# Twelve more weight panels of a decoder block as split float32r products, and convolution accumulators in PSUM

## The chip, the cores and the metric

The kernel runs on one core of a Trainium2 chip. The metric is the device time of one execution in microseconds; of the kernel before, three executions took 533.55, 533.61 and 533.82 us (median 533.61).

## What is computed

One layer of a hybrid decoder for 256 tokens of width 1024, in float32. A token mixer with two branches, then a mixture of experts:

```python
z = u @ w_in                                   # 1024 x 6144
u_rnn, u_gelu, c_val, c_gate, z_ga, z_gb = split(z)
h   = rg_lru(conv4(u_rnn), ...)                # 4-tap causal convolution, gates, linear recurrence
y_a = (h * gelu(u_gelu)) @ w_rnn_out
c   = conv31(c_val * sigmoid(c_gate))          # 31-tap causal depthwise convolution
y_b = silu(layer_norm(c)) @ w_conf_out
mixed = (sigmoid(z_ga) * y_a + sigmoid(z_gb) * y_b) @ w_out
```

After the mixer come a norm, a router (4 groups of 8 experts, top 2 in the best group) and 32 gated experts of width 256. The mixer is the first 265 us or so of the time, the router and the experts are the rest. The change is in the mixer.

## The kernel before

**Panels.** The mixer's weights are nine matrices of 1024 x 1024, each cut into four panels of 256 output channels, 36 panels `k` of 1 MB. Their order: 0 to 7 alternate between `c_val` (even) and `c_gate` (odd), then `K_RNN` 8 to 11, `K_GELU` 12 to 15, `K_GA` 16 to 19, `K_GB` 20 to 23, `K_YA` 24 to 27, `K_YB` 28 to 31, `K_WOUT` 32 to 35. A panel gives two output chunks `m` of 128 channels, each a sum over 8 blocks of 128 in a PSUM bank (`m % 4`), activation data transposed, 256 tokens as columns.

**Two ways to multiply.** A whole panel (`whole_panel`, L1057, matmuls on L1067) is 16 float32 matmuls of 256 columns, each of which is two records in the trace. A split panel (`split_panel`, `split_products`, L1076 to L1078) first needs its weights cut in two: ACT rounds them to float32r (`weight_hi`, L455, into slot `HI_SLOT + k % 4`), and DVE subtracts this from the original (`weight_lo`, L676, over the original in slot `MIX_SLOT + k % 4`). Then PE does three float32r matmuls in place of one: high by high, high weight by low operand, low weight by high operand. Panels 1, 2, 3 and 16 to 35 are split; 0 and 4 to 15 are whole, the latter in a loop of three turns.

**Loads.** SP issues the load of panel `k` (L328) once PE has finished panel `k - 4` (semaphore `pe_chunk`), since it goes into the same slot. Behind the loads of panels 8 and 10 it also issues expert weights (`load_unit`, four DMAs of 512 KB each time), which lie in slots of their own.

**ACT** evacuates the chunks in the order of the panels: conformer chunks into `cpad` and `gateA` (L448), then the first tap of the 31-tap convolution into `bufC` for two rounds' channels at a time (`first_taps`, L487), recurrence chunks into `bufA` with the first tap of the 4-tap one (L495, L497), gelu chunks into `bufG` (L465). Only at the gelu panels does it begin with the high halves of `K_GA`. After panel 16 come the 16 gate matmuls (`recurrence_gates`, L1109) in banks 4 to 7 in turn, each taken by ACT (L521).

**DVE** runs the 31-tap convolution with two channel blocks in turns (`conv`, L748), `acc = cpad * w + acc`, the accumulator in SBUF (`cacc`), the last tap back into `cpad`. Four rounds `i` of two blocks: rounds 0, 1 and 2 start from `bufC`, with the gating product of the next round (`gated`, L758) before tap 20. Then the 4-tap convolution of all eight blocks (also L748), the low halves of panels 16 and 17, and round 3 (whose tap 0 is L744) with three more low halves between its taps; then the recurrence, norm and more low halves. All of this is one fixed order.

**GpSimd** fills constants until 6.5 us and issues a few DMAs at 25 to 30 us. It does nothing else.

Of the kernel before, what the change touches and what calls it, by code (L numbers as in the profile page):

```python
# [18 lines left out]
F32 = mybir.dt.float32  # L19
# [3 lines left out]
ALU = mybir.AluOpType  # L23
ACT = mybir.ActivationFunctionType
ENG = mybir.EngineType
AX = mybir.AxisListType.X

P = 128
T = 256
TC = T // P  # L30
D = 1024
KC = D // P
CONVW = 31
# [12 lines left out]
PANEL = 2048  # L46
PN = PANEL // KC
SEG = D // PN
NMIX = 9 * SEG
# [9 lines left out]

K_RNN, K_GELU, K_GA, K_GB, K_YA, K_YB, K_WOUT = (n * SEG for n in range(2, 9))  # L60

SPLIT = [1, 2, 3] + list(range(K_GA, NMIX))
HI_SLOT, MIX_SLOT = SEG, 2 * SEG


R_GMIX, R_RCB, R_RCW, R_BR, R_BI, R_A, R_CCB, R_LNG, R_LNB, R_GFFN, R_CCW = 0, 1, 2, 6, 7, 8, 9, 10, 11, 12, 13
# [10 lines left out]
def build(nc, x, g_mix, w_in, rnn_conv_w, rnn_conv_b, lru_w_r, lru_b_r, lru_w_i, lru_b_i, lru_a_param,  # L77
# [4 lines left out]
    mixer_mem = ExitStack()  # L82

    def sb(name, shape, dt=F32, where=None):
        return (where or stack).enter_context(nc.sbuf_tensor(name, shape, dt))

    def loop(engine, lo, hi):

        return nc.Fori(lo, hi, engines=(engine,), hint_back_edge=True)

    def sem(name):
        return stack.enter_context(nc.semaphore(name))

    with stack:
# [36 lines left out]
        rdiag = bufD[:, 0, :].rearrange("p (t a) -> p t a", t=TC)  # L131
        lruw = gateB[:, :, :].rearrange("p (w a) (h j) -> p w (a h) j", w=2, h=2)
        lsc = sb("lsc", [P, 8, KC], F32, mixer_mem)
        cacc = sb("cacc", [P, 2, T], F32, mixer_mem)
        lnw = sb("lnw", [P, 3, T], F32, mixer_mem)
        mixer_mem.close()
        moe_mem = stack
# [46 lines left out]
        act_std = sem("act_std")  # L184
        act_whi = sem("act_whi")
        dve_wlo = sem("dve_wlo")
        act_split = sem("act_split")
        dve_split = sem("dve_split")
        act_lexp = sem("act_lexp")
# [4 lines left out]
        pe_chunk = sem("pe_chunk")  # L194
# [176 lines left out]
        def _(gp):  # L371
# [42 lines left out]
            gp.dma_start(brt[:, 0:NG], bcast(b_group_router, 0, P)).then_inc(router_in, 16)  # L414
            gp.dma_start(brt[:, NG:], bcast(b_expert_router, 0, P)).then_inc(router_in, 16)


        @block.scalar
        def _(act):
# [19 lines left out]
                act.activation(actT[:, c, :], ps[:, c % 4, c // 4 * T:(c // 4 + 1) * T], ACT.Copy,  # L439
                               scale=par[:, c, R_GMIX:R_GMIX + 1]).then_inc(act_evac, 1)  # L440

            def take_conformer(i):

                for b in range(4):
                    act.wait_ge(pe_chunk, i * 4 + (KC + b + 1))
                    c = bass.ds(i * 2 + b % 2, 1)
                    d = cpad[:, c, CONVW - 1:] if b < 2 else gateA[:, c, :]
                    act.activation(d.rearrange("p a b -> p (a b)"), ps[:, b, 0:T],  # L448
                                   ACT.Copy if b < 2 else ACT.Sigmoid).then_inc(act_evac, 1)

            def weight_hi(k):


                act.wait_ge(mixw_full[k % SEG], 16 * (k // SEG + 1))
                act.activation(ring_r[:, HI_SLOT + k % SEG, :], ring[:, MIX_SLOT + k % SEG, :], ACT.Copy  # L455
                               ).then_inc(act_whi, 1)

            def take_panel(k, func, dst, before=None):

                for m in (2 * k, 2 * k + 1):  # L460
                    c = m % KC
                    act.wait_ge(pe_chunk, KC + m + 1)
                    if before:
                        before(c)
                    act.activation(dst[:, c, 0:T], ps[:, m % 4, 0:T], func).then_inc(act_evac, 1)  # L465
# [18 lines left out]
            def first_taps(i):  # L484
                act.wait_ge(dve_cmul, i * 2 + 2)
                for c in (2 * i, 2 * i + 1):
                    act.activation(bufC[:, c, :], cpad[:, c, 0:T], ACT.Identity, scale=par[:, c, R_CCW:R_CCW + 1],  # L487
                                   bias=par[:, c, R_CCB:R_CCB + 1]).then_inc(act_ctap, 1)

            def take_rnn(i):  # L490

                for b in range(4):
                    c = i * 4 + b
                    act.wait_ge(pe_chunk, 3 * KC + c + 1)
                    act.activation(bufA[:, c, RNNW - 1:], ps[:, b, 0:T], ACT.Copy).then_inc(act_evac, 1)  # L495
                    act.wait_ge(act_evac, 3 * KC + c + 1)
                    act.activation(bufB[:, c, :], bufA[:, c, 0:T], ACT.Identity, scale=par[:, c, R_RCW:R_RCW + 1],  # L497
                                   bias=par[:, c, R_RCB:R_RCB + 1]).then_inc(act_tap, 1)

            act.wait_ge(gp_step, 7)  # L500
            take_conformer(0)
            first_taps(0)
            with loop(ENG.Activation, 1, SEG - 1) as i:
                take_conformer(i)
            first_taps(1)
            take_conformer(SEG - 1)
            first_taps(2)
            take_rnn(0)
            take_rnn(1)
            for p in range(SEG):  # L510
                if p >= 2:
                    weight_hi(K_GA + p - 2)
                take_panel(K_GELU + p, ACT.Gelu_apprx_tanh, bufG)
            weight_hi(K_GA + 2)
            take_ga(0)

            for m in range(2 * KC):
                c, w = m // 2, m % 2
                act.wait_ge(pe_lru, m + 1)
                row = (R_BR, R_BI)[w]  # L520
                act.activation((bufC, bufD)[w][:, c, :], ps[:, 4 + m % 4, 0:T], ACT.Sigmoid,  # L521
                               bias=par[:, c, row:row + 1]).then_inc(act_lru, 1)
            weight_hi(K_GA + 3)

# [137 lines left out]
        def _(v):  # L662
# [97 lines left out]

            def conformer_conv(lo, hi, before, **how):

                conv(lo, hi, cpad, lambda c, j: cacc[:, j:j + 1, :], lambda c, j: cpad[:, c, CONVW - 1:],
                     CONVW, R_CCW, R_CCB, before, dve_conv, **how)

            v.wait_ge(gp_step, 14)
# [261 lines left out]
        def _(pe):  # L1028
# [28 lines left out]
            def whole_panel(s, p, first=False):  # L1057

                pe.wait_ge(mixw_full[p], s * 16 + 16)
                w = slot_kn(ring, MIX_SLOT + p)  # L1060
                for m in (2 * p, 2 * p + 1):

                    pe.wait_ge(act_evac, s * KC + max(KC + m - 3, KC))
                    for k in range(KC):
                        if first:
                            pe.wait_ge(dve_u, k + 1)
                        last = pe.matmul(ps[:, m % 4, 0:T], w[:, k, (m % 2) * P:(m % 2 + 1) * P],  # L1067
                                         actT[:, k, :], start=(k == 0), stop=(k == KC - 1))
                    last.then_inc(pe_chunk, 1)
# [10 lines left out]

            def split_panel(k, x_hi, x_lo, before):

                pe.wait_ge(dve_wlo, SPLIT.index(k) + 1)
                w_hi, w_lo = slot_kn(ring_r, HI_SLOT + k % SEG), slot_kn(ring_r, MIX_SLOT + k % SEG)
                for m in (2 * k, 2 * k + 1):
                    before(m)
                    cols = slice((m % 2) * P, (m % 2 + 1) * P)
                    split_products(ps[:, m % 4, 0:T], lambda c: w_hi[:, c, cols], lambda c: w_lo[:, c, cols],
                                   lambda c: x_hi[:, c, 0:T], lambda c: x_lo[:, c, 0:T]).then_inc(pe_chunk, 1)
# [3 lines left out]

            whole_panel(0, 0, first=True)
            pe.wait_ge(dve_split, 1)
            for k in SPLIT[:3]:
                split_panel(k, u_hi, u_lo, evac_bank)
            with loop(ENG.PE, 1, K_GA // SEG) as s:
                for p in range(SEG):
                    whole_panel(s, p)  # L1100
            def recurrence_gates():
                pe.wait_ge(lruw_in, 32)
                for m in range(2 * KC):
                    c, w = m // 2, m % 2
                    if w == 0:
                        pe.wait_ge(dve_conv4, c + 1)
                    if m >= 4:
                        pe.wait_ge(act_lru, m - 3)
                    pe.matmul(ps[:, 4 + m % 4, 0:T], lruw[:, w, c, :], bufB[:, c, :], start=True, stop=True  # L1109
                              ).then_inc(pe_lru, 1)  # L1110

            def channel_sums(src, bank):
# [48 lines left out]
                return last  # L1161

            for p in range(SEG):
                pe.wait_ge(dve_wlo, SPLIT.index(K_WOUT + p) + 1)
                w_hi, w_lo = slot_kn(ring_r, HI_SLOT + p), slot_kn(ring_r, MIX_SLOT + p)
                for tc in range(TC):
                    if p:
                        pe.wait_ge(dve_h, 2 * (p - 1) + tc + 1)
                    tok = slice(tc * P, (tc + 1) * P)
                    split_products(ps[:, 4 + tc, 0:PN], lambda k: bufA_r[:, k, tok], lambda k: gateA_r[:, k, tok],  # L1170
                                   lambda k: w_hi[:, k, :], lambda k: w_lo[:, k, :],

                                   before=(lambda k: pe.wait_ge(dve_split, 4 + k + 1)) if p == tc == 0 else None
                                   ).then_inc(pe_wout, 1)
                if p >= 1:
                    h_transposes(p - 1)
                if p == 2:
                    pe.wait_ge(dve_gw, KC)
                if p >= 2:
                    logits(p - 2)  # L1180
# [163 lines left out]
```

## Time and profile before

| | us |
|---|---|
| median of the runs | 533.61 |
| span of the profiled execution, first to last instruction | 531.7 |
| PE busy, share of the span | 509.5, 96% |
| DVE busy | 273.2, 51% |
| ACT busy | 209.2, 39% |
| GpSimd busy | 9.6, 2% |

The total of the profiled execution is not listed beside its span; the median lies 1.9 us above the span. The page averages over the mixer and the experts; the windows and the order of time, which the rows below are from, show them apart. Matmul records overlap, since they are pipelined: their spacing, not their length, is what one costs. `issue` as a releaser means that the profile shows nothing that the engine waited for.

### The profile page before, as it was taken

The page shows a single profiled execution, that of the slowest core. Times are in us where ns is not written, and L with a number is a line of the kernel's source. Part 1 is how long each engine was busy: PE and PEld are TensorE (multiplying, and loading weights), DVE is VectorE, ACT ScalarE, POOL GpSimd, SP SyncE. Part 2 cuts the span into 40 slices and gives each one's busy share as a digit, 9 for nine tenths or more (in the row PEclk, how much of TensorE's full clock was granted, in tenths as well). Part 3 has the DMA queues.
Part 4 walks back from the last instruction along what each step waited for, and adds up shares of the span by engine and source line. Part 5 has one row for each costly group of instructions (what it writes and reads, how often), then busy time and mean ns, then how long its engine had stood idle before and what let it go on. Part 6 is the DMA issues. An engine that isn't in the chain of part 4 may idle for free.

```text
span 531.7 us, 8105 instructions
## 1 busy us (share of the span) xinstructions
PE 509.5 (96%) x2983; PEld 359.7 (68%) x2983; DVE 273.2 (51%) x550; ACT 209.2 (39%) x315; POOL 9.6 (2%) x25
## 2 busy tenths in 40 slices
PE   4999999999999999999989999999999999999994
PEld 4998888888999999999964353535435353534531
DVE  0589999969999996678282202221221212122123
ACT  2561113323897779345243231412323141322414
POOL 3020000000000000000000000000000000000000
PEclk8799999999999999999999999999999999999998
DMA  7594995434444438759996999999999999999932
GB/s 238 171 250 159 300 301 182 141 125 146 152 154 163 158 109 283 244 166 326 322 387 248 363 361 373 372 350 369 356 367 372 372 361 359 372 372 369 355 137 79
DMA packets 115970, 143.31 MB, mean 270 GB/s; under 512 B 3934, under 2 KB 106398, under 8 KB 115946
## 3 DMA queue, kind: packets, MB, share of 16 engines
q1 hardware_dynamic: 115502, 141.75, 79.5%
q0 software_dynamic: 432, 1.21, 0.8%
q8 instruction: 16, 0.26, 0.2%
q14 instruction: 8, 0.07, 0.0%
q10 hardware_dynamic: 12, 0.02, 0.0%
HBM read 141.90 MB, written 1.05 MB: 269 GB/s over the span
## 4 chain that ended last, share of the span: by engine, by line
PE 90%; DVE 4%; ACT 3%; DMA 2%; issue 1%; SPq 0%; DVEq 0%; ACTq 0%
PE ps L1267 21%; PE ps L1067 17%; PE ps L1304 11%; PE ps L1076 7%; PE ps L1078 7%; PE ps L1077 7%; PE ps L1219 6%; PE ps L1250 6%; DMA bufB<-in_conf_conv_b 2%; PE ps L1114 1%; PE ps L1109 1%; DVE ring_r L676 1%; PE ps L1032 1%; PE ps L1277 1%; PE ps L1286 1%; ACT bufC L565 1%
## 5 line engine op out<-in xcount | busy, mean ns | idle before, releaser
L1067 PE MATMUL ps<-actT,ring 128*128 128x256 f32 x416 | 90.8, 380 | 1.5 <-ACT gateA L448 1.0
L748 DVE SCALAR_TENSOR_TENSOR cacc<-cpad,par,cacc 128x256 f32<-128x256 f32 x226 | 90.3, 477 | 0.0
L1067 PEld LDWEIGHTS ps<-actT,ring 128*128 128x128 f32 x416 | 78.7, 190 | 13.1 <-ACT gateA L448 1.6
L1267 PE MATMUL ps<-ring,xslot 128*64 128x512 f32 x384 | 85.1, 594 | 0.0
L975 DVE SCALAR_TENSOR_TENSOR y_lo<-ps,wslot,y_hi 128x1024 fp32r<-128x1024 f32 x16 | 20.5, 1284 | 105.6 <-ACT y_hi L624 105.6
L1267 PEld LDWEIGHTS ps<-ring,xslot 128*64 128x64 f32 x384 | 27.0, 137 | 52.2 <-issue 51.4
L676 DVE TENSOR_TENSOR ring_r<-ring,ring_r 128x2048 fp32r<-128x2048 f32 x23 | 52.1, 2284 | 1.4 <-ACT ring_r L455 1.3
L1076 PE MATMUL ps<-u_hi,ring_r 128*128 128x256 f32 x176 | 50.4, 286 | 0.7 <-issue 0.7
L1077 PE MATMUL ps<-u_lo,ring_r 128*128 128x256 f32 x176 | 49.8, 283 | 0.0
L1078 PE MATMUL ps<-u_hi,ring_r 128*128 128x256 f32 x176 | 49.8, 283 | 0.0
L455 ACT ACTIVATE ring_r<-ring 128x2048 fp32r<-128x2048 f32 x23 | 43.7, 1907 | 8.4 <-DMA ring<-in_w_rnn_out 2.7
L987 DVE TENSOR_REDUCE wslot<-ps 64x1 f32<-64x2 f32 x32 | 5.1, 158 | 73.7 <-PE ps L1277 73.2
L638 ACT ACTIVATE sgate<-ps 128x256 f32<-128x256 f32 x16 | 6.1, 384 | 79.0 <-PE ps L1267 79.0
L1304 PE MATMUL ps<-ring,hidT 128*64 128x512 f32 x160 | 36.5, 598 | 0.0
L1076 PEld LDWEIGHTS ps<-u_hi,ring_r 128*128 128x128 f32 x176 | 33.8, 192 | 1.2 <-issue 1.1
L1077 PEld LDWEIGHTS ps<-u_lo,ring_r 128*128 128x128 f32 x176 | 33.8, 192 | 0.1
L1078 PEld LDWEIGHTS ps<-u_hi,ring_r 128*128 128x128 f32 x176 | 33.8, 192 | 0.0
L633 ACT ACTIVATE xslot<-ps 128x512 f32<-128x512 f32 x32 | 19.1, 598 | 37.1 <-PE ps L1250 37.1
L624 ACT ACTIVATE y_hi<-ps,wslot 128x1024 fp32r<-128x1024 f32 x16 | 17.8, 1111 | 35.7 <-PE ps L1304 35.7
L1267 PE MATMUL ps<-ring_high,xslot 128*64 128x512 f32 x128 | 28.6, 594 | 0.0
L1250 PE MATMUL ps<-sel,hn_hi 128*128 128x256 f32 x128 | 26.6, 289 | 1.3 <-DVE hn_lo L871 1.3
L1250 PE MATMUL ps<-sel,hn_lo 128*128 128x256 f32 x128 | 25.6, 282 | 0.0
(230 smaller groups left out, 775.6 us busy)
## 6 DMA issues: line engine op xcount, KB each, us to landing
ring<-in_w_in SPq DMA_DIRECT2D x24, 1024.0 KB, 5.2
ring<-in_w_gate SPq DMA_DIRECT2D x48, 512.0 KB, 8.8
ring<-in_w_up SPq DMA_DIRECT2D x48, 512.0 KB, 8.9
ring<-in_w_down SPq DMA_DIRECT2D x40, 512.0 KB, 8.1
ring_high<-in_w_gate SPq DMA_DIRECT2D x16, 512.0 KB, 8.9
ring_high<-in_w_up SPq DMA_DIRECT2D x16, 512.0 KB, 9.0
ring_high<-in_w_down SPq DMA_DIRECT2D x16, 512.0 KB, 8.2
ring<-in_w_rnn_out SPq DMA_DIRECT2D x4, 1024.0 KB, 4.9
```

The costliest lines, as they stand in the source:

```text
L455: act.activation(ring_r[:, HI_SLOT + k % SEG, :], ring[:, MIX_SLOT + k % SEG, :], ACT.Copy).then_inc(act_whi, 1)
L676: v.tensor_tensor(ring_r[:, MIX_SLOT + k % SEG, :], ring[:, MIX_SLOT + k % SEG, :], ring_r[:, HI_SLOT + k % SEG, :].bitcast(F32), ALU.subt ...
L748: ins = v.scalar_tensor_tensor(out=d if k == taps - 1 else a, in0=s, scalar=w, in1=start(c) if start and k == first else a, op0=ALU.mult, ...
L975: v.scalar_tensor_tensor(out=y_lo[:, :], in0=ps[:, 6:8, :].rearrange("p a b -> p (a b)"), scalar=wslot[:, pair:pair + 1], in1=y_hi[:, :].b ...
L1067: last = pe.matmul(ps[:, m % 4, 0:T], w[:, k, (m % 2) * P:(m % 2 + 1) * P], actT[:, k, :], start=(k == 0), stop=(k == KC - 1))
L1076: pe.matmul(dst, w_hi(k), x_hi(k), start=(k == 0), stop=False)
L1077: pe.matmul(dst, w_hi(k), x_lo(k), start=False, stop=False)
L1078: last = pe.matmul(dst, w_lo(k), x_hi(k), start=False, stop=(k == KC - 1))
L1219: last = pe.matmul(ps[:, 2 * tc + nn, :], selT[:, pair, tc * P:(tc + 1) * P], y[:, nn * 512:(nn + 1) * 512], start=False, stop=stop, skip_ ...
L1250: last = pe.matmul(ps[:, 4 + c // 2 % 2, c % 2 * T:(c % 2 + 1) * T], part[:, tc, c * P:(c + 1) * P], sel[:, tc, :], start=(t == 0), stop=( ...
L1267: last = pe.matmul(ps[SLOTS * j:SLOTS * (j + 1), 4, :], xslot[:, k, e * SLOTS:(e + 1) * SLOTS], w, start=(k == 0), stop=(k == KC - 1), ski ...
L1304: last = pe.matmul(ps[SLOTS * j:SLOTS * (j + 1), 6 + nn, :], hidT[:, f, SLOTS * j:SLOTS * (j + 1)], w[:, f, nn * 512:(nn + 1) * 512], star ...
```

## The change

Panels 4 to 15 become split panels. For them ACT makes the high half as for the others, and GpSimd the low half, in two instructions of 1024 columns each. ACT makes the high half of panel `k + 3` after it has evacuated panel `k`. PE's loop over the three groups of whole panels becomes straight code, as does ACT's loop over the conformer panels. The accumulators of the 31-tap convolution move from SBUF to bank 7 of PSUM, and the gate matmuls therefore take turns in banks 4 to 6. DVE's instructions and their order are the same otherwise.

```diff
-SPLIT = [1, 2, 3] + list(range(K_GA, NMIX))
+SPLIT = list(range(1, NMIX))
+
+POOL_LO = range(SEG, K_GA)
+DVE_LO = [k for k in SPLIT if k not in POOL_LO]
 HI_SLOT, MIX_SLOT = SEG, 2 * SEG
+GATE_BANKS, ACC_BANK = 3, 7
+WLO_PARTS = 2
...
-        cacc = sb("cacc", [P, 2, T], F32, mixer_mem)
...
+            for k in POOL_LO:
+                gp.wait_ge(act_whi, SPLIT.index(k) + 1)
+                for part in range(WLO_PARTS):
+                    cols = slice(part * PANEL // WLO_PARTS, (part + 1) * PANEL // WLO_PARTS)
+                    gp.tensor_tensor(ring_r[:, MIX_SLOT + k % SEG, cols], ring[:, MIX_SLOT + k % SEG, cols],
+                                     ring_r[:, HI_SLOT + k % SEG, cols].bitcast(F32), ALU.subtract
+                                     ).then_inc(gp_wlo, 1)
...
             act.wait_ge(gp_step, 7)
-            take_conformer(0)
-            first_taps(0)
-            with loop(ENG.Activation, 1, SEG - 1) as i:
-                take_conformer(i)
-            first_taps(1)
-            take_conformer(SEG - 1)
-            first_taps(2)
-            take_rnn(0)
-            take_rnn(1)
-            for p in range(SEG):
-                if p >= 2:
-                    weight_hi(K_GA + p - 2)
-                take_panel(K_GELU + p, ACT.Gelu_apprx_tanh, bufG)
-            weight_hi(K_GA + 2)
+            for k in range(K_GA):
+                if k < K_RNN:
+                    take_conformer(k)
+                elif k < K_GELU:
+                    take_rnn(k - K_RNN)
+                else:
+                    take_panel(k, ACT.Gelu_apprx_tanh, bufG)
+                if k == 1:
+                    first_taps(0)
+                if k == 5:
+                    first_taps(1)
+                if k == K_RNN + 2:
+                    first_taps(2)
+                if k >= 1:
+                    weight_hi(k + 3)
             take_ga(0)
...
-                conv(lo, hi, cpad, lambda c, j: cacc[:, j:j + 1, :], lambda c, j: cpad[:, c, CONVW - 1:],
+                def conv_acc(j):
+                    return ps[:, ACC_BANK, j * T:(j + 1) * T].rearrange("p (a b) -> p a b", a=1)
+                conv(lo, hi, cpad, lambda c, j: conv_acc(j), lambda c, j: cpad[:, c, CONVW - 1:],
                      CONVW, R_CCW, R_CCB, before, dve_conv, **how)
...
-                pe.wait_ge(dve_wlo, SPLIT.index(k) + 1)
+                if k in POOL_LO:
+                    pe.wait_ge(gp_wlo, WLO_PARTS * (POOL_LO.index(k) + 1))
+                else:
+                    pe.wait_ge(dve_wlo, DVE_LO.index(k) + 1)
...
-            for k in SPLIT[:3]:
+            for k in range(1, K_GA):
                 split_panel(k, u_hi, u_lo, evac_bank)
-            with loop(ENG.PE, 1, K_GA // SEG) as s:
-                for p in range(SEG):
-                    whole_panel(s, p)
...
-                    if m >= 4:
-                        pe.wait_ge(act_lru, m - 3)
-                    pe.matmul(ps[:, 4 + m % 4, 0:T], lruw[:, w, c, :], bufB[:, c, :], start=True, stop=True
+                    if m >= GATE_BANKS:
+                        pe.wait_ge(act_lru, m - GATE_BANKS + 1)
+                    pe.matmul(ps[:, 4 + m % GATE_BANKS, 0:T], lruw[:, w, c, :], bufB[:, c, :], start=True, stop=True
                               ).then_inc(pe_lru, 1)
```

## Rows read from the trace of the kernel before

**Rows 1.** The page: busy us, share of the span, instructions of each engine.
```profile
PE 509.5 (96%) x2983; PEld 359.7 (68%) x2983; DVE 273.2 (51%) x550; ACT 209.2 (39%) x315; POOL 9.6 (2%) x25
```

**Rows 2.** Chain of waits in order of time: start us, us, what.
```profile
46.55 27.91 PE ps L1067 x128
...
74.92 27.91 PE ps L1067 x128
...
103.28 27.89 PE ps L1067 x128
```

**Rows 3.** Windows after the twelve panels: busy us (instructions), granted clock, DMA share, GB/s.
```profile
130.00:140.00 10.00, 10.00 (x70) 9.48 (x68) 10.00 (x18) 6.85 (x12) 0.00 (x0) 1.00 0.50 159
...
sum 70.00, PE 69.97 PEld 67.97 DVE 68.72 ACT 55.60 POOL 0.00; mean PE 10.00 PEld 9.71 DVE 9.82 ACT 7.94 POOL 0.00
```

**Rows 4.** Order of time on DVE: start us, us, what, [idle before <-releaser].
```profile
37.77 0.88 DVE L748 SCALAR_TENSOR_TENSOR cacc<-cpad,par,bufC 128x256 f32<-128x256 f32 x2 [1.16 <-ACT bufC L487]
...
63.50 14.33 DVE L748 SCALAR_TENSOR_TENSOR cacc<-cpad,par,cacc 128x256 f32<-128x256 f32 x36
...
111.22 0.87 DVE L748 SCALAR_TENSOR_TENSOR cpad<-cpad,par,cacc 128x256 f32 x2
117.08 10.26 DVE L748 SCALAR_TENSOR_TENSOR bufB<-bufA,par,bufB  x24 [4.99 <-issue]
127.26 4.49 DVE L676 TENSOR_TENSOR ring_r<-ring,ring_r 128x2048 fp32r<-128x2048 f32 x2
```

**Rows 5.** Order of time on ACT: ends of panels 1, 3, 15, and two gates.
```profile
34.51 0.38 ACT L448 ACTIVATE gateA<-ps 128x256 f32<-128x256 f32 x1 [1.46 <-PE ps L1078]
...
46.11 0.38 ACT L448 ACTIVATE gateA<-ps 128x256 f32 x1 [2.49 <-PE ps L1078]
...
131.21 0.39 ACT L465 ACTIVATE bufG<-ps 128x256 f32<-128x256 f32 x1 [3.07 <-PE ps L1067]
...
137.40 0.47 ACT L521 ACTIVATE bufC<-ps,par 128x256 f32<-128x256 f32 x1
137.83 0.48 ACT L521 ACTIVATE bufD<-ps,par 128x256 f32<-128x256 f32 x1
```

**Rows 6.** PE's early pause, and windows around it, columns as in rows 3.
```profile
5.01 2.56 PE L1040 MATMUL ps<-ident,hres 128*128 128x128 f32 x16
13.79 1.08 PE L1046 MATMUL ps<-ident,bufB 44*128 44x44 f32 x8 [6.22 <-DMA bufB<-in_conf_conv_b]
...
10.00:12.00 2.00, 0.00 (x0) 0.00 (x0) 0.00 (x0) 0.00 (x0) 0.00 (x0) 0.50 0.91 276
...
18.00:20.00 2.00, 2.00 (x11) 2.00 (x11) 1.35 (x4) 0.56 (x2) 0.00 (x0) 0.51 1.09 354
20.00:22.00 2.00, 2.00 (x15) 1.85 (x14) 1.97 (x8) 0.12 (x1) 0.00 (x0) 1.00 0.28 91
```

**Rows 7.** Order of time on DVE, operations with SBUF and PSUM inputs.
```profile
276.21 1.39 DVE L871 SCALAR_TENSOR_TENSOR hn_lo<-hg,stat,hn_hi 128x512 fp32r<-128x512 f32 x2
...
516.17 0.42 DVE L990 TENSOR_TENSOR hid<-sgate,ps 128x256 f32<-128x256 f32 x1
516.51 0.75 DVE L928 TENSOR_TENSOR sel<-rank,iota_s 128x256 fp32r<-128x256 f32 x2
...
525.87 1.41 DVE L1022 SCALAR_TENSOR_TENSOR hres<-ps,stat,gfin 128x512 f32<-128x512 f32 x2
```

**Rows 8.** GpSimd in order of time; DVE beside its DMA issues; ACT's high halves.
```profile
3.97 1.49 POOL L397 TENSOR_SCALAR selT<-ones 128x512 fp32r<-128x512 f32 x1
...
26.38 0.90 POOL L411 DMA_DIRECT2D gateB<-in_lru_w_i  x1
...
26.10 6.69 DVE L676 TENSOR_TENSOR ring_r<-ring,ring_r 128x2048 fp32r<-128x2048 f32 x3
...
L455 ACT ACTIVATE ring_r<-ring 128x2048 fp32r<-128x2048 f32 x23 | 43.7, 1907 | 8.4 <-DMA ring<-in_w_rnn_out 2.7
```

**Rows 9.** DMA queues in 114 to 115 us: packets, MB, share.
```profile
q14 instruction: 1, 0.01, 2.3%
```

**Rows 10.** DMA issues of weight panels: count, KB each, median us to landing.
```profile
ring<-in_w_in SPq DMA_DIRECT2D x24, 1024.0 KB, 5.2
```

More of the change, by code:

```diff
@@ L186, in build @@
         dve_wlo = sem("dve_wlo")
+        gp_wlo = sem("gp_wlo")
         act_split = sem("act_split")
@@ L440, in _, with take_conformer @@
                                scale=par[:, c, R_GMIX:R_GMIX + 1]).then_inc(act_evac, 1)
[L442 to L449, printed above, removed]
+            def take_conformer(k):
+                for j in range(2):
+                    c = k // 2 * 2 + j
+                    act.wait_ge(pe_chunk, KC + 2 * k + j + 1)
+                    d = cpad[:, c, CONVW - 1:] if k % 2 == 0 else gateA[:, c, :]
+                    act.activation(d, ps[:, (2 * k + j) % 4, 0:T], ACT.Copy if k % 2 == 0 else ACT.Sigmoid
+                                   ).then_inc(act_evac, 1)
             def weight_hi(k):
@@ L490, in take_rnn @@
             def take_rnn(i):
-                for b in range(4):
-                    c = i * 4 + b
+                for c in (2 * i, 2 * i + 1):
+                    b = c % 4
                     act.wait_ge(pe_chunk, 3 * KC + c + 1)
@@ L520, in _ @@
                 row = (R_BR, R_BI)[w]
-                act.activation((bufC, bufD)[w][:, c, :], ps[:, 4 + m % 4, 0:T], ACT.Sigmoid,
+                act.activation((bufC, bufD)[w][:, c, :], ps[:, 4 + m % GATE_BANKS, 0:T], ACT.Sigmoid,
                                bias=par[:, c, row:row + 1]).then_inc(act_lru, 1)
@@ L1163, in _ @@
             for p in range(SEG):
-                pe.wait_ge(dve_wlo, SPLIT.index(K_WOUT + p) + 1)
+                pe.wait_ge(dve_wlo, DVE_LO.index(K_WOUT + p) + 1)
                 w_hi, w_lo = slot_kn(ring_r, HI_SLOT + p), slot_kn(ring_r, MIX_SLOT + p)
```

## Prediction

> **What bounds the kernel now.** I read the page first [rows 1]: PE is busy 509.5 of 531.7 us, DVE 273.2. An average over two quite different halves says little, so I next took the chain of waits for the mixer half [rows 2]: three blocks of 27.9 us of float32 matmuls (L1067) follow one another, 46.55 to 131.2, and each is four of the twelve panels that the change touches. After them PE goes on without a pause: in the seven windows from 130 to 200 us it is busy 69.97 of 70.00 us [rows 3]. So PE is the bound from 28.5 us on. The question is who is second, and how far behind. DVE's order of time [rows 4] answers it: DVE is convolving without a gap from 37.8 to 112.1 us, has one gap of 4.99 us, does the 4-tap convolution to 127.3, then the low half of panel K_GA (L676), and its other windows up to 190 us are full too [rows 3]. DVE is a second chain, running beside PE and almost as long.
>
> **The twelve panels.** Panel 15, the last float32 one, is evacuated at 131.21; panel 3, the last split one, at 46.11; panel 1 at 34.51 [rows 5]. So twelve float32 panels take 85.1 us, and one split panel takes (46.11 - 34.51) / 2 = 5.80 us. Twelve split panels would take 69.6 us, and PE would have finished panel 15 at 46.1 + 69.6 = 115.7 instead of 131.2: 15.5 us less work.
>
> **Who ends the wait for panel K_GA.** The first thing PE needs next is the low half of panel K_GA, and DVE makes it, after its convolutions, in an order that the diff leaves alone. DVE's first L676 of that pair starts at 127.26 and takes 2.28 us: 129.5 [rows 4]. Nothing on DVE's way there is taken off it: the twelve new low halves are GpSimd's, but the old kernel did not have them at all. DVE also waits for nobody on that way who becomes faster, since its only idle time there is the 4.99 us with no releaser. So PE can start K_GA at 129.5, only 131.2 - 129.5 = 1.7 us earlier; the other 13.8 us of the saving become a wait. Term one: -1.7 us.
>
> **What the wait itself costs.** At the start of the kernel PE stops at 7.57 us, and the granted clock is 0.50 from 10 us on; PE resumes at 13.79 and has the full clock only from about 20.0 [rows 6]. That is a level of 1.2 GHz instead of 2.4 for 6.2 us of work, which loses 3.1 us. A wait of 13.8 us is longer than that pause of 6.2, so panel K_GA and the first gates would run at the lower level. Behind them PE was full already [rows 3], so nothing absorbs it. Bounds 0 and 3.1; I take 3.1, the row. Term two: +3.1 us.
>
> **What happens to DVE's convolution.** Three pieces.
> - Accumulators in PSUM. Up to 112.1 us DVE issues 174 operations that write the accumulator (29 taps, 2 channels, 3 rounds), spaced (14.34 - 0.48) / 35 = 0.396 us [rows 4]. No row has DVE writing to PSUM. As a source, PSUM costs a scalar_tensor_tensor of 512 columns 12 ns: two in a row take 1.41 us from PSUM and 1.39 with both inputs in SBUF, and single ones 746 against 738 ns; the tensor_tensor of 256 columns with a PSUM input is followed after 0.34 us, as those from SBUF are [rows 7]. So 0 to 12 ns on the input side, I take 6: 1.0 us. The output side is bounded by the two spacings that this engine shows at 256 columns, 0.34 and 0.40: one operation could be 60 ns shorter (-10 us) or, as far again the other way, 60 ns longer (+10 us). A result has to be written either way; I take nothing.
> - Meeting GpSimd. GpSimd would now read and write SBUF for 60 us beside DVE. The trace has no such overlap: GpSimd computes until 6.5 us, and what it does at 26 to 30 us are DMA issues, beside which DVE's 2048-column subtractions take their usual 2.2 us each [rows 8]. Lower bound 0. Upper bound: DVE operations with both inputs in SBUF wait out whatever GpSimd instruction is running. While GpSimd works there are five such pairs (the gating at taps 20 of three rounds, and the first tap from bufC in two). GpSimd's only 512-column arithmetic takes 1.49 us [rows 8], so half a panel is at least 2.98 us, and catching it half way costs 1.5 us: 7.5 us. I take 3, a little under the middle.
> - The gap of 4.99 us. An instruction packet lands in 114 to 115 us on the queue that fetched for DVE [rows 9], with a weight load under way; this is code, and its length stays. Between 0 and -5 us; I take 0.
>
> Term three: +1.0 + 3.0 = +4.0 us.
>
> **What is hidden.** Everything that feeds the twelve panels has 13.8 us of cover. ACT's twelve more high halves cost it 1.9 us of each 5.8 [rows 8], beside two evacuations of 0.38 [rows 5]. Weight loads land in 5.2 us at the median, under the 5.8 of a panel [rows 10]; the two unit loads of 2 MB, which SP issues behind the loads of K_RNN and K_RNN + 2, push the next panel load back some 6 us each, and the cover takes that. PE's unrolled code is straight-line, as in K_GA to K_GB, where it runs at full rate [rows 3]. The gates' banks go from four to three: ACT takes one gate each 0.43 us at 0.47 us a piece [rows 5], PE needs 0.43, so a bank is back after 0.90 of the 1.29 us that three give. If there is no wait before K_GA (DVE much faster) these would begin to show, at most 2 us.
>
> GpSimd is cover-dependent too. Its first low half can start at 39.6 (ACT free at 37.7, 1.9 for the high half); it is hidden while 39.6 + 12p + 5.8 is under 133.5, that is while a panel takes it p < 7.3 us. From the row above p is at least 4 x 1.49 = 5.96, and twice that if a second input costs as much as the first. The Trainium skill, GPSIMD Engine Reference, Performance versus the Vector engine, gives 4497 ns for a float32 tensor_tensor of 2048 columns; by it GpSimd would keep up even with 5.8 us a panel. That row of 1.49 us for a quarter of the columns doesn't agree well with it.
>
> **Sum.** -1.7 + 3.1 + 4.0 = +5.4 us. Of the profiled execution, whose span is 531.7, that makes 537.1; its own total isn't listed, and the median of the runs is 1.9 above the span, so 533.6 + 5.4 = 539.0 us. From K_GA on PE is late by 5.4 and DVE by 4.0 (+0.4 for 58 further PSUM operations), so PE stays the bound and hands the whole of it to the expert half.
>
> **Rivals.**
> - A, faster: DVE reaches K_GA earlier. The place is the 174 operations; it decides as soon as terms two and three together are below +1.7, so with no meeting cost when an operation gets over 8 ns shorter (1.4 / 174). With 20 ns (-3.5), 2 us off the code gap and nothing lost to GpSimd: 1.4 - 5.5 = -4.1, 529.5 us. For: the gap depends on what is in the DMA queues, and 0.34 us is shown for an operation of that length. Against: PSUM rows are never shorter. 0.20.
> - B, GpSimd bounds. At 9 us a panel (between 5.96 and 11.9) the last low half is at 39.6 + 108 = 147.6, PE starts K_GA at 153.4, +22.2: 555.8 us. For: the 1.49 us row. 0.12.
> - C, the convolution keeps its pace and GpSimd does not disturb it: 1.4 us, 535.0. For: the tensor_tensor rows. 0.15, half of it inside 0.2%.
> - D, full exclusion: 1.4 + 1.0 + 7.5 = +9.9, 543.5 us. DVE's paired operations wait for whole GpSimd halves, five times. 0.13.
>
> By the Trainium skill, SBUF — State Buffer, Who interferes with whom, a VectorE instruction with two SBUF inputs and a GpSimd instruction that reads SBUF exclude each other, and the later one waits for the whole instruction; one with a single SBUF input does not. By that rule it would be D, and the accumulators in PSUM would spare the other taps. No row here shows it.
>
> **The numbers.** My own sum 0.40, A 0.20, B 0.12, C 0.15, D 0.13. A measurement of this kernel tells changes above 0.2% (1.1 us). Slower: 0.40 + 0.12 + 0.13 + 0.07 = 0.72; the same 0.08; faster 0.20. The range goes down to 530, which holds half of A, and up to 548, which holds D and a convolution some 50 ns slower an operation, and leaves B out.
>
> **What would show it.** PE idle before K_GA for 10 us or more, ended by DVE ring_r L676 (step one), with the granted clock at 0.5 for some 6 us after (step two). DVE's spacing in the convolution, 0.396 us or other; longer first taps or gatings while POOL is busy (step three). POOL's time for half a panel: over 3.6 us is B. I am wrong if DVE's first low half of K_GA comes before 128 us, or if the clock holds through the wait.

## The result and the profile after

The changed kernel took 540.04 us (median of four runs, 539.01 to 543.72) against 533.58 us in the same session: ratio 1.0125, 95% interval 1.0104 to 1.0146. It is slower, by 6.5 us; 539.0 was forecast. The profiled execution took 540.59 us with a span of 538.5, 6.8 us above the span of before.

The page of the changed kernel, first part and the rows of the slices for PE, GpSimd and the clock:

```profile
PE 499.6 (93%) x3175; PEld 358.7 (67%) x3175; DVE 278.5 (52%) x550; ACT 230.4 (43%) x327; POOL 67.3 (12%) x49
...
PE   4999999950999999999999999999999999999994
...
POOL 3139779800000000000000000000000000000000
PEclk8799999995899999999989999999999999999999
```

PE has 10 us less to do than in [rows 1] and the kernel is longer: for half of slice 9 and nearly all of slice 10 PE stands idle, and the granted clock falls to a half. The waits name who ended that:

```profile
PE ps L1092 <- DVE ring_r L690: 19.7, 2, 19.1
```

One wait of 19.1 us for a low half from DVE. Line numbers are higher by 13 to 16 now: L690 is the low half on DVE, L762 the taps, L772 the gating, L468 the high half. The order of time on DVE, which answers [rows 4]:

```profile
52.70 1.81 DVE L772 TENSOR_TENSOR cpad<-cpad,gateA 128x256 f32<-128x256 f32 x2
...
63.55 2.73 DVE L762 SCALAR_TENSOR_TENSOR ps<-cpad,par,bufC 128x256 f32 x2 [0.42 <-DVE cpad L762]
66.20 14.19 DVE L762 SCALAR_TENSOR_TENSOR ps<-cpad,par,ps 128x256 f32<-128x256 f32 x36
...
90.04 3.81 DVE L762 SCALAR_TENSOR_TENSOR ps<-cpad,par,bufC 128x256 f32 x2 [0.38 <-DVE cpad L762]
...
121.99 10.25 DVE L762 SCALAR_TENSOR_TENSOR bufB<-bufA,par,bufB  x24 [4.75 <-issue]
132.16 4.48 DVE L690 TENSOR_TENSOR ring_r<-ring,ring_r 128x2048 fp32r<-128x2048 f32 x2
```

Taps with the accumulator in PSUM take 14.19 us for 36, where [rows 4] has 14.33. But pairs of operations with both inputs in SBUF take up to 3.81 us; in the kernel before such a pair took 0.75 (gating) or 0.88 us (first taps). I call what a pair takes above that what it lost: here 1.06, 1.85 and 2.93, together 5.8 us. The other two of the five pairs fell into stretches in which GpSimd had nothing to do. DVE comes to its low halves at 132.16 instead of 127.26. ACT's evacuations, which answer [rows 5]: ends of panels 1, 3, 15 and K_GA, and K_YA:

```profile
34.56 0.38 ACT L461 ACTIVATE gateA<-ps 128x256 f32<-128x256 f32 x1 [1.46 <-PE ps L1094]
...
46.08 0.38 ACT L461 ACTIVATE gateA<-ps 128x256 f32<-128x256 f32 x1 [2.50 <-PE ps L1094]
...
115.44 0.38 ACT L478 ACTIVATE bufG<-ps 128x256 f32<-128x256 f32 x1 [2.49 <-PE ps L1094]
...
142.92 0.38 ACT L478 ACTIVATE gateA<-ps 128x256 f32<-128x256 f32 x1 [2.52 <-PE ps L1094]
...
202.82 0.39 ACT L478 ACTIVATE bufD<-ps 128x256 f32<-128x256 f32 x1 [2.24 <-PE ps L1094]
```

Panel 15 is finished at 115.44, K_GA at 142.92 (136.96 before), K_YA at 202.82 (197.05 before). GpSimd in order of time, with its 24 new instructions:

```profile
39.65 14.25 POOL L426 TENSOR_TENSOR ring_r<-ring,ring_r 128x1024 fp32r<-128x1024 f32 x6 [9.40 <-ACT ring_r L468]
54.11 5.04 POOL L426 TENSOR_TENSOR ring_r<-ring,ring_r 128x1024 fp32r<-128x1024 f32 x2 [0.21 <-ACT ring_r L468]
```

14.25 us for six is 2.38 us a half panel, under the 2.98 that was forecast as its least. And the clock, which answers [rows 6] (columns as in [rows 3]):

```profile
118.00:120.00 2.00, 0.00 (x0) 0.00 (x0) 0.00 (x0) 0.93 (x1) 0.00 (x0) 0.86 0.95 332
120.00:122.00 2.00, 0.00 (x0) 0.00 (x0) 0.01 (x1) 0.00 (x0) 0.00 (x0) 0.50 0.01 2
...
138.00:140.00 2.00, 2.00 (x12) 2.00 (x11) 2.00 (x6) 0.00 (x0) 0.00 (x0) 0.52 0.00 0
140.00:142.00 2.00, 2.00 (x18) 2.00 (x18) 2.00 (x3) 0.39 (x1) 0.00 (x0) 1.00 0.00 0
```

PE resumed at 134.5 and had 1.2 GHz until 140, 5.5 us.

Of the 6.8 us, 5.8 are there at K_YA (202.82 against 197.05) and still at the router's logits (273.15 against 267.40). The last 1.1 us arise behind them, in 273 to 277 us, where eight matmuls on the residual take 4.96 instead of 3.59 us, the granted clock being 0.50 there:

```profile
274.00:275.00 1.00, 1.00 (x2) 0.40 (x2) 0.83 (x7) 1.00 (x1) 0.00 (x0) 0.50 0.99 290
```

The kernel before had 1.00 in the same stage of its profile. I have no experiment on this dip, and its cause stays open. But it isn't the new panels that bring it: the kernel before with nothing changed but its accumulators and gate banks (second experiment) shows it in its profile, and two kernels with the new panels (quarters with pauses, and the same with 80 matmuls on constants) do not:

```profile
268.00:270.00 2.00, 2.00 (x5) 1.19 (x5) 1.61 (x11) 1.98 (x2) 0.00 (x0) 0.51 0.96 311
```

### The profile page after: what moved, and what is told of

It reads as the page before. It is cut to its first block, busy times and chain, and to the rows that moved or that the text cites. A ratio compares the mean times of both kernels' runs of the same rounds, so it can differ in the third digit from the quotient of the medians.

```text
span 538.5 us, 8483 instructions
## 1 busy us (share of the span) xinstructions
PE 499.6 (93%) x3175; PEld 358.7 (67%) x3175; DVE 278.5 (52%) x550; ACT 230.4 (43%) x327; POOL 67.3 (12%) x49
## 4 chain that ended last, share of the span: by engine, by line
PE 70%; DVE 16%; issue 6%; ACT 3%; DMA 2%; DVEq 2%; SPq 0%
PE ps L1283 21%; PE ps L1320 11%; DVE ps L762 9%; PE ps L1092 6%; PE ps L1235 6%; PE ps L1093 6%; PE ps L1094 6%; PE ps L1266 6%; DVE ring_r L690 3%; DMA bufB<-in_conf_conv_b 2%; PE ps L1125 1%; PE ps L1130 1%; DVEq L761 1%; PE ps L1293 1%; PE ps L1212 1%
## 5 line engine op out<-in xcount | busy, mean ns | idle before, releaser
L1092 PE MATMUL ps<-u_hi,ring_r 128*128 128x256 f32 x368 | 106.0, 288 | 19.6 <-DVE ring_r L690 19.1
L1094 PE MATMUL ps<-u_hi,ring_r 128*128 128x256 f32 x368 | 105.2, 286 | 0.0
L1093 PE MATMUL ps<-u_lo,ring_r 128*128 128x256 f32 x368 | 105.2, 286 | 0.0
L762 DVE SCALAR_TENSOR_TENSOR ps<-cpad,par,ps 128x256 f32<-128x256 f32 x226 | 89.4, 479 | 0.0
L1092 PEld LDWEIGHTS ps<-u_hi,ring_r 128*128 128x128 f32 x368 | 71.8, 195 | 20.4 <-DVE ring_r L690 19.3
L468 ACT ACTIVATE ring_r<-ring 128x2048 fp32r<-128x2048 f32 x35 | 66.5, 1907 | 15.3 <-DMA ring<-in_w_in 8.5
L1093 PEld LDWEIGHTS ps<-u_lo,ring_r 128*128 128x128 f32 x368 | 71.8, 195 | 0.1
L1094 PEld LDWEIGHTS ps<-u_hi,ring_r 128*128 128x128 f32 x368 | 71.7, 195 | 0.0
L426 POOL TENSOR_TENSOR ring_r<-ring,ring_r 128x1024 fp32r<-128x1024 f32 x24 | 57.7, 2443 | 17.7 <-ACT ring_r L468 17.7
L690 DVE TENSOR_TENSOR ring_r<-ring,ring_r 128x2048 fp32r<-128x2048 f32 x23 | 52.1, 2284 | 0.5 <-ACT ring_r L468 0.4
L647 ACT ACTIVATE xslot<-ps 128x512 f32<-128x512 f32 x32 | 19.1, 598 | 37.0 <-PE ps L1266 37.0
L1266 PEld LDWEIGHTS ps<-sel,hn_hi 128*128 128x128 f32 x128 | 19.6, 189 | 7.2 <-issue 7.2
```

The lines of the kernel that those rows point to most:

```text
L426: gp.tensor_tensor(ring_r[:, MIX_SLOT + k % SEG, cols], ring[:, MIX_SLOT + k % SEG, cols], ring_r[:, HI_SLOT + k % SEG, cols].bitcast(F32) ...
L690: v.tensor_tensor(ring_r[:, MIX_SLOT + k % SEG, :], ring[:, MIX_SLOT + k % SEG, :], ring_r[:, HI_SLOT + k % SEG, :].bitcast(F32), ALU.subt ...
L762: ins = v.scalar_tensor_tensor(out=d if k == taps - 1 else a, in0=s, scalar=w, in1=start(c) if start and k == first else a, op0=ALU.mult, ...
L1092: pe.matmul(dst, w_hi(k), x_hi(k), start=(k == 0), stop=False)
L1093: pe.matmul(dst, w_hi(k), x_lo(k), start=False, stop=False)
L1094: last = pe.matmul(dst, w_lo(k), x_hi(k), start=False, stop=(k == KC - 1))
```

## The experiments

Twelve kernels. Times are medians; a ratio is to the kernel before in the same session, with its 95% interval.

**Accumulators in SBUF again.** The changed kernel with this undone:

```diff
+        cacc = sb("cacc", [P, 2, T], F32, mixer_mem)
-                conv(lo, hi, cpad, lambda c, j: conv_acc(j), ...
+                conv(lo, hi, cpad, lambda c, j: cacc[:, j:j + 1, :], ...
```

> The changed kernel with the 31-tap accumulators back in SBUF, GpSimd still making the twelve low halves. Theory (a DVE operation with both inputs in SBUF and a GpSimd instruction exclude each other, for the length of the instruction): every tap now has two SBUF inputs, so nearly each of GpSimd's 24 instructions of 2.4 us holds DVE up once. DVE's convolution gets some 50 us longer while GpSimd works, K_GA starts that much later, 580 to 595 us. Rival (the 5.8 us that the five pairs lost have another cause, such as the start of a tensor_tensor): the taps keep 0.39 us and the time stays within 2 us of 540.

583.18 us, ratio 1.0919 (1.0896 to 1.0943). The theory held: DVE comes to its 4-tap convolution 44 us later than in the changed kernel (166.28 against 121.99). DVE and GpSimd in order of time:

```profile
38.46 14.34 DVE L763 SCALAR_TENSOR_TENSOR cacc<-cpad,par,cacc 128x256 f32<-128x256 f32 x36
...
53.39 29.32 DVE L763 SCALAR_TENSOR_TENSOR cacc<-cpad,par,cacc 128x256 f32<-128x256 f32 x20
...
41.15 32.24 POOL L427 TENSOR_TENSOR ring_r<-ring,ring_r 128x1024 fp32r<-128x1024 f32 x8 [10.64 <-ACT ring_r L469]
```

One detail was not in the theory. From 41.15 GpSimd had work, yet DVE's 36 taps went on at full pace to 52.8 us, and GpSimd's first instruction took 14.53 us. Then the engines took turns: DVE's next 20 taps took 29.3 instead of 8 us, and taken singly, 24 operations of DVE waited behind GpSimd's 24 instructions, one behind each. So DVE's stream of short operations kept GpSimd out, but GpSimd's stream of long ones did not keep DVE out. The first eight GpSimd instructions took 32.2 us in place of 19.

**Accumulators in PSUM alone.** The kernel before with them in bank 7 and the gates in three banks:

```diff
+GATE_BANKS, ACC_BANK = 3, 7
-                conv(lo, hi, cpad, lambda c, j: cacc[:, j:j + 1, :], ...
+                conv(lo, hi, cpad, lambda c, j: conv_acc(j), ...
-                    pe.matmul(ps[:, 4 + m % 4, 0:T], ...
+                    pe.matmul(ps[:, 4 + m % GATE_BANKS, 0:T], ...
```

> The kernel before with the accumulators in PSUM bank 7 and the gates in three banks, nothing else. Theory: taps are 4 ns shorter each (14.19 against 14.33 us for 36), DVE reaches K_GA 0.7 us earlier, PE is the bound there and nothing moves: 533.6 within 0.3 us. Rival: three gate banks or PSUM writes cost something by themselves: 534.5 to 536.

533.89 us, ratio 0.9996 (0.9984 to 1.0008). Taps 14.19 us for 36 in each round, so it is PSUM and not GpSimd's company that makes them 4 ns shorter. Neither that nor the three banks moves the time.

**Matmuls on constants in the wait**, to keep the clock up. This was tried four times, until it bridged the wait:

```diff
+            keep_warm(80)
+
             def recurrence_gates():
```

> The changed kernel with 80 float32 matmuls of 128 columns on constants between panel 15 and K_GA, 17 us of work in a wait of 19. Theory (the wait costs the clock): granted clock 1.00 through K_GA, panel K_GA takes 5.8 instead of 8.4 us, 537.3 us. Rival (the clock stretch is absorbed behind): 540 as before.

540.46 us, ratio 1.0106 (1.0057 to 1.0156): undecided. In the profiled run DVE's pairs lost 10.8 us instead of 5.8, PE began K_GA at 138.5, the constants ended at 133.5, and the clock had fallen again. The runs lay between 538.3 and 543.1: what the pairs lose differs from run to run, and had to be made steady first.

**Length of GpSimd's instructions.** One of 2048 columns a panel, and eight of 256:

```diff
-WLO_PARTS = 2
+WLO_PARTS = 1      # and, in the next kernel, 8
```

> The changed kernel with GpSimd's low half as one instruction of 2048 columns per panel (some 4.7 us) instead of two of 2.4. Theory (DVE's pairs with two SBUF inputs wait for the end of the running instruction): what they lose grows with the instruction's length, from 5.8 and 10.8 us in the two profiles of two halves to 10 to 18 us; 544 to 552 us, with a wide spread. Rival (a fixed cost for each meeting): 538 to 543 as with two halves.

552.25 us, ratio 1.0341 (1.0326 to 1.0356). The time is 0.3 us above the expected range; 20.4 us were lost in the pairs, where 10 to 18 were expected.

> The changed kernel with GpSimd's low half as eight instructions of 256 columns. Theory: no pair waits more than some 0.7 us an operation, together 2 to 4 us instead of 5.8 to 10.8, the low half of K_GA comes near 131, and the time is 535.5 to 538 us with a spread under 2 us. Rival (a fixed cost for each meeting, or as many more meetings as the instructions are shorter): 540 or more. GpSimd may need some 0.1 to 0.2 us more an instruction, up to 6 us a panel, which PE's wait covers.

549.22 us (543.83 to 550.12), ratio 1.0283 (1.0268 to 1.0298). Missed: short instructions are hardly better than long ones. With one instruction a panel, the two operations of a pair on DVE and GpSimd's instructions beside them, taken singly:

```profile
82.76 3.31 DVE L772 TENSOR_TENSOR cpad<-cpad,gateA  x1
85.99 4.84 DVE L772 TENSOR_TENSOR cpad<-cpad,gateA  x1
...
81.16 4.63 POOL L426 TENSOR_TENSOR ring_r<-ring,ring_r 128x2048 fp32r<-128x2048 f32 x1 [2.79 <-ACT ring_r L468]
85.75 4.80 POOL L426 TENSOR_TENSOR ring_r<-ring,ring_r 128x2048 fp32r<-128x2048 f32 x1
```

GpSimd's instructions end at 85.79 and 90.55, DVE's operations at 86.07 and 90.83. Each operation of the pair waits for the end of the instruction that is running when it comes: the first for what is left of one, the second, since GpSimd has begun again meanwhile, for a whole further one. In the changed kernel, with halves, it is the same. GpSimd's instructions beside this pair end at 91.03 and 93.57:

```profile
90.04 1.27 DVE L762 SCALAR_TENSOR_TENSOR ps<-cpad,par,bufC 128x256 f32 x1 [0.38 <-DVE cpad L762]
91.23 2.62 DVE L762 SCALAR_TENSOR_TENSOR ps<-cpad,par,bufC 128x256 f32 x1
```

In the five profiles with instructions of 1024 or 2048 columns 46 operations waited, and all 46 ended 0.28 to 0.30 us after the first end of a GpSimd instruction that came behind their start. With eight:

```profile
52.55 9.97 DVE L772 TENSOR_TENSOR cpad<-cpad,gateA 128x256 f32<-128x256 f32 x1
...
39.83 22.40 POOL L426 TENSOR_TENSOR ring_r<-ring,ring_r 128x256 fp32r<-128x256 f32 x32 [9.77 <-ACT ring_r L468]
```

An instruction takes 0.70 us, and DVE's operation nevertheless took 9.97. It let 13 ends of instructions pass and ended at 62.52, where GpSimd's stream of 32, for four panels without a break, had ended at 62.23. The other four waits of this profile were one instruction long. So behind short instructions an operation sometimes waits until GpSimd's stream pauses; what decides whether it does, no run shows. With eight, a panel takes GpSimd 5.6 us, as long as a panel of PE, and pauses become rare. My theory fell in this point. The profiled execution was the fastest of the five, 543.83 us; the next kernel's profile shows what the others may have lost.

> As the kernel with eight instructions a panel, and 62 float32 matmuls of 128 columns on constants (13.6 us) between panel 15 and K_GA. With the short instructions K_GA's low half should come within 2 us of the last of them, before the clock falls. Theory (the wait costs 2.7 to 3.1 us of clock): 2.5 to 3 us less than that kernel without them, 533 to 535 us. Rival (the stretch is absorbed): the same time as without them.

549.87 us, ratio 1.0277 (1.0244 to 1.0310). Two operations waited to the end of GpSimd's streams, 10.36 and 7.06 us; the pairs lost 17.7 us, so it doesn't tell of the clock.

**A pause behind each instruction.** Quarters, and GpSimd waits for its own semaphore:

```diff
-WLO_PARTS = 2
+WLO_PARTS = 4
                                      ).then_inc(gp_wlo, 1)
+                    gp.wait_ge(gp_wlo, WLO_PARTS * POOL_LO.index(k) + part + 1)
```

> The changed kernel with four instructions a panel on GpSimd, and GpSimd waiting for its own semaphore after each, so that its stream pauses. Theory formed on the traces of one and of eight instructions a panel (DVE's two-input operation waits until GpSimd's back-to-back stream pauses, 9.7 us in one case, not until the running instruction ends): with a pause behind each instruction of 1.26 us no pair loses more than 1.3 us an operation, together 3 to 6 us, against 5.8 to 10.8 in halves and 11 to 16 in eighths; 536 to 540 us with a small spread. Rival (many short instructions are themselves what costs): 544 to 550 us, as with eighths. GpSimd needs 5.4 to 5.8 us a panel.

539.51 us, ratio 1.0101 (1.0086 to 1.0117), all four runs between 539.01 and 539.84. The time is as the theory had it; the pairs:

```profile
52.60 2.61 DVE L773 TENSOR_TENSOR cpad<-cpad,gateA 128x256 f32<-128x256 f32 x2
...
64.25 2.09 DVE L763 SCALAR_TENSOR_TENSOR ps<-cpad,par,bufC 128x256 f32 x2 [0.42 <-DVE cpad L763]
...
90.10 2.28 DVE L763 SCALAR_TENSOR_TENSOR ps<-cpad,par,bufC 128x256 f32 x2 [0.38 <-DVE cpad L763]
...
39.84 27.65 POOL L426 TENSOR_TENSOR ring_r<-ring,ring_r 128x512 fp32r<-128x512 f32 x20 [9.73 <-ACT ring_r L469]
```

GpSimd is at work for 27.65 us with hardly a gap, and yet no pair loses more than 1.9 us. Together they lose 6.3, a little above what I expected, and the four runs lie within 0.8 us. This run changed the length and the pause together, and by itself it doesn't show what the pause does: a wait of one instruction of 1.3 us an operation would look the same without it. The pair of kernels that differs in the pause alone comes last.

> The same, with 66 float32 matmuls of 128 columns on constants (14.5 us) between panel 15 and K_GA. Theory (the wait costs clock): granted clock 1.00 at the start of K_GA and 2.5 to 3 us less than without them. Rival (absorbed): no difference.

539.93 us, ratio 1.0102 (1.0086 to 1.0117). The constants ended at 130.6, the clock was at 0.50 from 134 on, K_GA came at 134.9: not bridged, so the last run used 80.

> The kernel with four instructions a panel, the pause behind each, and 80 instead of 66 matmuls on constants before K_GA: with 66 the last of them ended at 130.6 us, the clock fell near 133.7, and K_GA came at 134.9, so that run did not bridge the wait. 80 of 0.223 us end at 133.7, 1.2 us before K_GA. Theory (the wait costs clock): granted clock 1.00 through K_GA, its panel in 5.8 instead of 8.2 to 8.4 us, and 2.4 to 3 us less than the 539.5 us without them: 536.5 to 537.2. Rival (the stretch at the lower level is absorbed behind): 539 to 540.

538.96 us, ratio 1.0100 (1.0084 to 1.0117), against 1.0101 without the constants. The wait was bridged this time:

```profile
134.00:136.00 2.00, 1.11 (x9) 1.11 (x10) 2.00 (x2) 0.00 (x0) 0.00 (x0) 1.00 0.00 0
136.00:138.00 2.00, 2.00 (x19) 2.00 (x19) 2.00 (x4) 0.00 (x0) 0.00 (x0) 1.00 0.00 0
```

The rival is right for this kernel: the stretch at the lower clock is absorbed. ACT's evacuations at K_GA and K_YA with the clock held, and then without (the kernel of the pauses alone):

```profile
140.94 0.38 ACT L479 ACTIVATE gateA<-ps 128x256 f32<-128x256 f32 x1 [2.49 <-PE ps L1095]
...
202.36 0.38 ACT L479 ACTIVATE bufD<-ps 128x256 f32<-128x256 f32 x1 [1.82 <-PE ps L1095]
```

```profile
142.48 0.38 ACT L479 ACTIVATE gateA<-ps 128x256 f32<-128x256 f32 x1 [2.49 <-PE ps L1095]
...
202.37 0.39 ACT L479 ACTIVATE bufD<-ps 128x256 f32<-128x256 f32 x1 [1.96 <-PE ps L1095]
```

PE is 1.54 us ahead at K_GA and 0.01 at K_YA. With the clock held it waits 0.8 us on the way, for ACT's squares of the layer norm, which ACT makes from DVE's subtraction of the mean. This subtraction in the kernel before, the changed kernel, with 66 and with 80 matmuls, and then K_GA and K_YA with 66:

```profile
183.32 2.29 DVE L812 TENSOR_TENSOR cpad<-cpad,lnw 128x2048 f32<-128x2048 f32 x1
...
188.21 2.30 DVE L828 TENSOR_TENSOR cpad<-cpad,lnw 128x2048 f32<-128x2048 f32 x1
...
188.63 2.29 DVE L829 TENSOR_TENSOR cpad<-cpad,lnw 128x2048 f32<-128x2048 f32 x1
...
188.61 2.29 DVE L829 TENSOR_TENSOR cpad<-cpad,lnw 128x2048 f32<-128x2048 f32 x1
...
143.34 0.39 ACT L479 ACTIVATE gateA<-ps 128x256 f32<-128x256 f32 x1 [2.51 <-PE ps L1095]
...
203.23 0.39 ACT L479 ACTIVATE bufD<-ps 128x256 f32<-128x256 f32 x1 [2.25 <-PE ps L1095]
```

Two chains meet at K_YA. In ten of the fourteen profiles, the kernel before and the one with 80 matmuls among them, K_YA comes 13.73 to 13.77 us after the start of DVE's subtraction. In the other four, the changed kernel, the quarters with pauses without constants and with 66, and the eighths with constants, it comes later than that, and 59.89 or 59.90 us after K_GA. So the later of the two decides. With 66 and 80 matmuls DVE is equally late, and the low clock costs 0.87 us at K_YA; without constants the two chains are 0.14 us apart, and it costs that. The times of these three kernels, 539.93, 538.96 and 539.51 us, overlap in their runs and do not tell so small a cost.

**DVE relieved of low halves.** If DVE's order is what bounds, work must leave DVE. GpSimd also takes panels K_GA to K_GA + 4, most of them made while DVE's taps have only one input in SBUF. The gate matmuls move behind K_GA + 1, since they need the 4-tap convolution:

```diff
-POOL_LO = range(SEG, K_GA)
+POOL_LO = range(SEG, K_GA + 5)
...
-            weight_lo(K_GA + 0)
-            weight_lo(K_GA + 1)
...
-            conformer_conv(3, 4, input_and_sums, between={5: lambda i: weight_lo(K_GA + 2), ...
+            conformer_conv(3, 4, input_and_sums)
...
-                if k == K_GA:
+                if k == K_GA + 1:
                     recurrence_gates()
```

> The changed kernel, with the low halves of K_GA to K_GA + 4 on GpSimd too (17 panels instead of 12), so that DVE makes none before the recurrence, and the gate matmuls behind panel K_GA + 1 instead of K_GA. Theory (DVE's order is what ends the wait): DVE is relieved of five times 2.2 us, PE starts K_GA near 116, the gates wait for the 4-tap convolution (122 to 132), and DVE's chain behind is 6 us ahead of the kernel before: 527 to 529 us. Rival (GpSimd's further 24 us collide with the 4-tap convolution, whose operations have two SBUF inputs): DVE loses what it was relieved of, 533 to 540.

529.72 us (528.98 to 531.08), ratio 0.9922 (0.9898 to 0.9946): faster than both kernels, 0.7 us short of the expected range. DVE, then ACT's end of K_GA and of K_YA:

```profile
123.20 10.26 DVE L762 SCALAR_TENSOR_TENSOR bufB<-bufA,par,bufB  x24 [3.55 <-issue]
...
134.28 22.80 DVE L762 SCALAR_TENSOR_TENSOR ps<-cpad,par,ps 128x256 f32<-128x256 f32 x58
...
120.81 0.38 ACT L478 ACTIVATE gateA<-ps 128x256 f32<-128x256 f32 x1 [1.88 <-PE ps L1091]
...
192.16 0.38 ACT L478 ACTIVATE bufD<-ps 128x256 f32<-128x256 f32 x1 [1.80 <-PE ps L1091]
```

K_GA ends at 120.81 instead of 142.92, and round 3 of the convolution runs without low halves between. At K_YA the kernel is 4.9 us ahead of the one before, 13.74 us behind DVE's subtraction of the mean: DVE's chain decides there. Its pairs lost 8.5 us. The 4-tap convolution kept its 10.26 us, since GpSimd did nothing between 122.1 and 137.5.

> The kernel with 17 panels on GpSimd and the gates behind panel K_GA + 1, with four instructions of 512 columns a panel instead of two of 1024. Theory: its DVE lost 8.3 us to GpSimd in the profile with halves; with quarters it loses 3 to 5, and as DVE's order bounds the mixer up to the norm, the time falls by 3 to 5 us, to 525 to 527. Rival (PE or the weight loads bound it by now): 529 to 530, as with halves.

533.77 us (528.18 to 537.87), ratio 0.9967 (0.9941 to 0.9994). Missed; the pairs lost 10.8 us in the profile, 5.7 of them in one: its first operation took 5.00 us, past three ends of quarters, to a pause of GpSimd. The spread of 9.7 us may come from such waits; with one profile for twelve runs it is not shown.

> The kernel with 17 panels on GpSimd and the gates behind panel K_GA + 1, with four instructions a panel and the pause behind each. Theory: DVE's chain loses 3 to 5 us to GpSimd instead of 8.3 (halves) or 11 (quarters without a pause), and bounds the mixer up to the norm: 524 to 527 us, in a narrower spread than the 528 to 538 of the quarters without a pause. Rival (PE bounds by now): 529 to 530.

530.88 us (530.05 to 531.37), ratio 0.9931 (0.9918 to 0.9945). Against the quarters without a pause it is steadier, and no operation took over 1.52 us: this is what the pause does. In the four profiles with it 36 operations waited, each for one instruction. But it is not faster than with halves: the pairs lost 6.6 us, and the 4-tap convolution 2.1 (12.35 us for its 24 operations instead of 10.26), since GpSimd, slower with pauses, was still on a low half then. Expected was 524 to 527 and a loss of 3 to 5 us; the loss to GpSimd is 8.7 against 8.5 with halves, so nothing was won. K_YA is 1.6 us later than with halves, of which 1.1 is DVE's gap without a releaser (4.69 against 3.55 us).

## Why the prediction came out right, and which steps did not

- **Twelve panels take 69.6 us** and panel 15 ends at 115.7: it ended at 115.44. Right.
- **DVE's low half ends the wait** and not PE, ACT, GpSimd or a load: right, 19.1 us of waiting with that name on it, and moving the low half away turned the loss into a gain (0.9922).
- **Accumulators in PSUM, +1.0 us**: mis-sized, the other sign. 36 taps went from 14.33 to 14.19, 174 operations from some 69 to 68.3 us, -0.7. I had bounded the output side on both sides and taken nothing.
- **Meeting GpSimd, +3.0 us**: the largest term that was mis-sized. It was 5.8 us in the profile, and 10.8 in another run of the same GpSimd code. The trace of before could not show it. The mechanism of the bound, waiting out the running instruction, was right, but the upper bound of 7.5 was none: it took half an instruction a pair. A pair is two operations, and the second meets a whole further instruction (1.27 and 2.62 us in the changed kernel, where alone each takes 0.48). Two pairs of the other run lost 4.2 and 4.3 us each.
- **Code gap, 0**: 4.75 us instead of 4.99; it was 3.54 to 5.70 over the kernels.
- **GpSimd's speed**: 4.8 us a panel, below the 5.96 that was taken as its least from one row of a different instruction. Rival B was never near; the 4497 ns of the Trainium skill (GPSIMD Engine Reference, Performance versus the Vector engine) was the better guide, the trace nearly agreeing with 4.62 us for one instruction of 2048 columns.
- **PE's wait and the low clock, -1.7 + 3.1 us**: PE began K_GA 3.3 us later than before, the 4.9 of DVE less the 1.7; panel K_GA then took 2.7 us longer at the low clock. It ends 5.96 us late (142.92 against 136.96).
- **"PE stays the bound"**: this held in the changed kernel, by less than 1 us, near the margin of 1.0 that the forecast has between 5.4 and 4.4. At K_YA PE's chain is 5.8 us late and DVE's subtraction of the mean 4.9. What I had wrong is that DVE had slack: at K_GA it was 1.7 us early before, at K_YA it was already the later one, by 0.2 us (K_YA came 60.09 us behind K_GA, where PE by itself needs 59.90), though PE was busy all along. So "nothing absorbs it" is right for the sum and wrong for the clock by itself: of its 2.7 us only 0.9 are on top of what DVE would have cost anyway.

So the sum of the mixer was predicted as +1.4 + 4.0 and measured as some +0.9 + 4.9: convolution -0.7, pairs +5.8, gap -0.2, and 0.9 that PE is later than DVE. The last 1.1 us are the clock dip at the router, which no step of mine had. The two terms of DVE's convolution erred in opposite directions, by 1.7 and 2.8 us; the closeness of 539.0 to 540.04 is partly luck.

By the Trainium skill (SBUF — State Buffer, Who interferes with whom) the two engines exclude each other when both read SBUF as here, and one SBUF input is free of it. The runs agree: 583.18 us with the accumulators in SBUF, and taps undisturbed at 14.19 with them in PSUM. That the later one waits for the whole instruction, the traces agree with for halves and whole panels (46 of 46 waits); behind instructions of 0.70 and 1.25 us four operations waited longer, up to 14 ends of instructions. Rival D was right in kind and its price too small.

## What to carry to other kernels

Before taking work off the busiest engine, list who hands it its next operand, and how long that engine has been running without a gap: a second chain just 1.7 us behind left 1.7 us of a 15.5 us saving here, before what the change itself added. Slack read at one point of a chain isn't slack at the next. An engine that comes as a helper may stop the one that it was meant to spare, so count the operations that share a resource with it, and place the helper's work where the other needs only one SBUF input. Count operations and not pairs: each may wait for an instruction of its own.

## What the runs showed of the hardware

- DVE operations with two SBUF inputs and GpSimd subtractions don't overlap. Beside GpSimd instructions of 2.38 and 4.62 us each operation of DVE ended 0.28 to 0.30 us after the running instruction, 46 times of 46. A stream of short ones can keep the other engine out: 9.9 us of waiting behind instructions of 0.70 us each, 5.0 behind quarters of 1.25, and GpSimd behind DVE's taps of 0.4 us, 14.53 us for an instruction that takes 2.4. With a wait on its own semaphore behind each of GpSimd's instructions none of 36 operations waited for more than one, at 0.12 us an instruction (1.37 us from start to start, against 1.25 without).
- GpSimd subtracts float32 to float32r at 2.38 us for 1024 columns, 4.62 for 2048, 0.70 for 256.
- A DVE tap with accumulator in PSUM both ways is 4 ns shorter than in SBUF, at 256 columns.
- The granted clock fell some 4 us after PE stopped (115.4 to between 118 and 120), in other runs after some 3 (with 66 constants, 130.6 to between 132 and 134) to 5 us (with 80 in the first try, 133.5 to between 138 and 139). It was full again 5.5 us after PE resumed, with quarters and pauses less than 5.3 (134.8 to between 138 and 140).
